# Filter network of the long convolution: its own transfer semaphore, sample columns on two partition halves, weight sums on GpSimd, modulation steps behind the first units

## What is computed

```python
def implicit_filter_fft(length, w1, b1, w2, b2, w3, freq):
    z = jnp.concatenate([t, jnp.cos(bands * w), -jnp.sin(bands * w)], axis=-1)      # length x 33
    hid = jnp.sin(fr * (z @ w1 + b1))
    hid = jnp.sin(fr * (hid @ w2 + b2))
    filt = (hid @ w3).reshape(length, 2, HYENA_ORDER, D_HYENA)
    filt = filt * window[:, None, None, :]
    fwd, bwd = filt[:, 0], filt[:, 1]
    two_sided = jnp.concatenate([fwd, zeros, bwd[1:][::-1]], axis=0)
    two_sided = two_sided / jnp.sum(jnp.abs(two_sided), axis=0, keepdims=True)
    return jnp.fft.rfft(two_sided, axis=0)

def ada_mod(cond, w_ada, b_ada):
    return jnp.split(jax.nn.silu(cond) @ w_ada + b_ada, N_MOD, axis=-1)             # 1024 x 6144
```

## Time and profile before

| | |
|---|---|
| median of 3 runs | 3439.83 us (3432.54 to 3440.22) |
| the profiled execution | 3434.03 us, span 3432.1 us |
| TensorE busy, share of the span | 3190.5 us, 93% |
| VectorE busy | 2245.4 us, 65% |
| ScalarE busy | 1697.3 us, 49% |
| GpSimd busy | 397.4 us, 12% |
| the chain that ended last | matmuls of the experts' stage, from the end back |
| last instruction of the `filters` stage | ends near 350 us |
| first matmul of `projection` | 351.66 us |

### The profile page before, as it was taken

The page is one execution under the profiler, slowest core; times in us unless marked ns, Lnnn a source line. Parts: engine busy times, 40 slices in busy tenths (PEclk is TensorE's granted clock), DMA queues, the critical chain, the costliest instruction groups (busy, mean ns, idle before and its releaser), DMA issues.

```text
span 3432.1 us, 54507 instructions
## 1 busy us (share of the span) xinstructions
PE 3190.5 (93%) x22416; PEld 2468.7 (72%) x22416; DVE 2245.4 (65%) x2850; ACT 1697.3 (49%) x2194; POOL 397.4 (12%) x326
## 2 busy tenths in 40 slices
PE   4879799979899894999999999999999999999996
PEld 2546688868787783777777777777777777777774
DVE  6765423247766637777777777777777777777766
ACT  2222422136511322666666666666666666666664
POOL 1320010011155032000000000000000000000010
PEclk8789899989999996999999999999999999999998
DMA  3455262245378424677877787788778777777785
GB/s 133 162 188 188 102 164 87 79 126 141 142 267 277 144 92 166 261 284 288 294 277 287 278 295 276 272 296 288 275 289 296 273 291 293 275 292 274 277 332 199
DMA packets 226036, 791.15 MB, mean 231 GB/s; under 512 B 28526, under 2 KB 35322, under 8 KB 221565
## 3 DMA queue, kind: packets, MB, share of 16 engines
q1 hardware_dynamic: 206028, 722.02, 57.0%
q0 software_dynamic: 19760, 65.65, 6.7%
HBM read 730.31 MB, written 57.26 MB: 229 GB/s over the span
## 4 chain that ended last, share of the span: by engine, by line
PE 58%; DMA 1%; DVE 1%; ACT 0%; issue 0%; POOL 0%; SPq 0%; ACTq 0%; POOLq 0%; DVEq 0%
PE exp_bank L2860 15%; PE exp_bank L2862 14%; PE exp_bank L2861 14%; PE exp_bank L2870 14%; PE exp_bank L2842 1%; DMA out_y<-exp_xb 1%; PE exp_bank L2844 1%; DMA exp_xb<-residual 0%; PE exp_bank L2828 0%; DVE g_pick L2423 0%; DVE g_pick L2422 0%; DVE g_pick L2425 0%; DVE exp_lo L2556 0%; DMA exp_xq<-hidden_rows,g_rows_q 0%; PE exp_bank L2832 0%
## 5 line engine op out<-in xcount | busy, mean ns | idle before, releaser
L2556 DVE TENSOR_TENSOR exp_lo<-exp_raw,exp_hi 128x1024 fp32r<-128x1024 f32 x1056 | 1277.0, 1223 | 251.2 <-ACT exp_hi L2552 193.6
L2552 ACT ACTIVATE exp_hi<-exp_raw 128x1024 fp32r<-128x1024 f32 x1056 | 1119.4, 1062 | 570.7 <-PE exp_bank L2862 558.0
L2860 PE MATMUL exp_bank<-exp_hi,exp_xt 128*128 128x512 f32 (+1 forms) x1536 | 588.8, 383 | 1.6 <-DVE exp_xt L2709 1.0
L2862 PE MATMUL exp_bank<-exp_hi,exp_xt 128*128 128x512 f32 (+1 forms) x1536 | 572.1, 372 | 0.0
L2861 PE MATMUL exp_bank<-exp_lo,exp_xt 128*128 128x512 f32 (+1 forms) x1536 | 571.7, 372 | 0.0
L2860 PEld LDWEIGHTS exp_bank<-exp_hi,exp_xt 128*128 128x128 f32 x1536 | 289.5, 189 | 87.5 <-issue 39.1
L2862 PEld LDWEIGHTS exp_bank<-exp_hi,exp_xt 128*128 128x128 f32 x1536 | 289.8, 189 | 52.0
L2870 PE MATMUL exp_bank<-exp_raw,exp_xtp 128*32 128x256 f32 (+1 forms) x6144 | 324.1, 363 | 0.0
L2861 PEld LDWEIGHTS exp_bank<-exp_lo,exp_xt 128*128 128x128 f32 x1536 | 290.3, 189 | 45.5
L2860 PE MATMUL exp_bank<-exp_hi,exp_hid 128*128 128x512 f32 x704 | 283.3, 402 | 10.4 <-DVE exp_lo L2556 10.4
L2870 PEld LDWEIGHTS exp_bank<-exp_raw,exp_xtp 128*32 128x32 f32 x6144 | 185.1, 110 | 127.0 <-issue 30.9
(11 more groups left out here) (414 smaller groups left out, 4568.6 us busy)
## 6 DMA issues: line engine op xcount, KB each, us to landing
exp_raw<-in_w SPq DMA_DIRECT2D x1056, 512.0 KB, 6.5
hy_table<-in_basis_s POOLq DMA_DIRECT2D x64, 512.0 KB, 4.7
carry_tiles<-in_w_ada SPq DMA_DIRECT2D x24, 1024.0 KB, 5.4
proj_raw<-in_w_in SPq DMA_DIRECT2D x24, 512.0 KB, 4.6
filt_raw<-in_kbasis_s SPq DMA_DIRECT2D x18, 512.0 KB, 6.1
spectrum_s<-filt_spec SPq DMA_DIRECT2D x34, 256.0 KB, 2.2
carry_flex<-spectrum_s SPq DMA_DIRECT2D x16, 512.0 KB
features<-proj_xr SPq DMA_DIRECT2D x12, 512.0 KB, 3.0
```

What stands on the lines that cost most here:

```text
L2552: act.activation(st.hi[:, n % st.ns, :], raw(n), ACT.Copy).then_inc(st.hi_done, 1)
L2556: dve.tensor_tensor(st.lo[:, n % st.ns, :], raw(n), st.hi[:, n % st.ns, :].bitcast(F32), ALU.subtract).then_inc(st.lo_done, 1)
L2860: pe.matmul(out, xh, wh, start=(k == 0), stop=False)
L2862: mm = pe.matmul(out, xl, wh, start=False, stop=(k == nk - 1))
```

## The change

- Six transfers (`z`, `w1`, the biases twice, `w2` twice) go first and count on `s_net` of their own, `cond` on `s_cond`; then `w3`, then the other nine on `s_in`.
- `w2` has its two copies one below the other, [128, 64] for [64, 128]. The network's prompt columns stay on 64 partitions in both layers. The sample columns' first 512 go to partitions 0 to 63, the last 512 to partitions 64 to 127, so each step covers 512 elements on 128 partitions. ScalarE puts them back beside each other in the second layer's sine, and copies by three blocks.
- GpSimd forms `wsum` and rows 0 to 63 of `W2`; ScalarE makes the zeros of `W2` by a copy with scale 0.
- TensorE's steps ahead of `gen(0)` are gone from there: one stands behind `gen(0)`, one behind `gen(1)`, two ahead of `gen(2)`. VectorE's: one behind `larger(0)`, one behind `larger(1)`, and as before one behind `inverse(0)`. All later calls are as before.
- SP waits for six sines instead of four ahead of the `skip` loads.

```diff
-        w1, w2 = ph.sb("w1", [33, 64]), ph.sb("w2", [64, 128])
+        w1, w2 = ph.sb("w1", [33, 64]), ph.sb("w2", [128, 64])
...
-            sp.dma_start(z, a["z"]).then_inc(s_in, 16)
-            sp.dma_start(w1[:], a["filt_w1"]).then_inc(s_in, 16)
+            sp.dma_start(z, a["z"]).then_inc(s_net, 16)
+            sp.dma_start(w1[:], a["filt_w1"]).then_inc(s_net, 16)
             for x in range(2):
-                sp.dma_start(w2[:, 64 * x:64 * x + 64], a["filt_w2"]).then_inc(s_in, 16)
-                sp.dma_start(fb[64 * x:64 * x + 64, :], a["filt_b"]).then_inc(s_in, 16)
-            for dst, name in ((cond, "cond"), (bada, "bada"), (g["gains"], "gains"), (g["ident"], "ident"), (sel, "sel"), (sgn_f, "sgn")):
+                sp.dma_start(fb[64 * x:64 * x + 64, :], a["filt_b"]).then_inc(s_net, 16)
+            for x in range(2):
+                sp.dma_start(w2[64 * x:64 * x + 64, :], a["filt_w2"]).then_inc(s_net, 16)
+            sp.dma_start(cond[:], a["cond"]).then_inc(s_cond, 16)
+            for x in range(2):
+                sp.dma_start(w3[64 * x:64 * x + 64].rearrange("p d o f -> p (d o f)"), a["filt_w3"]).then_inc(s_w3, 16)
+            for dst, name in ((bada, "bada"), (g["gains"], "gains"), (g["ident"], "ident"), (sel, "sel"), (sgn_f, "sgn")):
                 sp.dma_start(dst[:], a[name]).then_inc(s_in, 16)
             for x, s in enumerate("ps"):
                 sp.dma_start(wmid[:, x, :], a[f"wmid_{s}"]).then_inc(s_in, 16)
                 sp.dma_start(rowf[:, x, :], a[f"rowf_{s}"]).then_inc(s_in, 16)
-            for x in range(2):
-                sp.dma_start(w3[64 * x:64 * x + 64].rearrange("p d o f -> p (d o f)"), a["filt_w3"]).then_inc(s_w3, 16)
...
-            sp.wait_ge(s_sin, 4)
+            sp.wait_ge(s_sin, 6)
...
+            def hidden_p(layer):
+                if layer:
+                    pe.wait_ge(s_sin, 1)
+                pe.matmul(pf[0][0:64, 0:ZS - ZP], w2[0:64] if layer else w1[:], (hid[0:64] if layer else z)[:, ZP:ZS],
+                          start=True, stop=True).then_inc(s_h, 1)
+
+            def hidden_s(layer):
+
+                for h in range(2):
+                    rows, out = slice(64 * h, 64 * h + 64), pf[1 + layer][64 * h:64 * h + 64, :]
                     if layer:
-                        pe.wait_ge(s_sin, 1 if b == 0 else 2)
-                    pe.matmul(pf[b][0:128 if layer else 64, 0:c1 - c0], (w2 if layer else w1)[:],
-                              (hid[0:64] if layer else z)[:, c0:c1], start=True, stop=True).then_inc(s_h, 1)
+                        pe.wait_ge(s_sin, 2)
+                        mm = pe.matmul(out, w2[rows], hid[rows, ZS:ZS + 512], start=True, stop=True)
+                    else:
+                        mm = pe.matmul(out, w1[:], z[:, ZS + 512 * h:ZS + 512 * h + 512], start=True, stop=True)
+                mm.then_inc(s_h, 1)
...
-            pe.wait_ge(s_in, 16 * 16)
-            hidden(0, (0, 1, 2))
-            ada(2)
-            hidden(1, (0,))
-            hidden(1, (1, 2))
+            pe.wait_ge(s_net, 16 * 6)
+            hidden_p(0)
+            hidden_s(0)
+            hidden_p(1)
+            hidden_s(1)
+            pe.wait_ge(s_in, 16 * 9)
+            gen(0)
             ada()
-            gen(0)
             gen(1)
+            ada()
             sums(0)
             middles()
             close(0)
-            ada()
+            ada(2)
             gen(2)
...
-            act.wait_ge(s_in, 16 * 16)
-            act.activation(sgn[:], sgn_f[:], ACT.Copy)
+            act.wait_ge(s_cond, 16)
             act.activation(sc[:], cond[:], ACT.Silu).then_inc(s_silu, 1)
-            for layer in range(2):
-                for b, (c0, c1) in enumerate(((ZP, ZS), (ZS, ZN))):
-                    act.wait_ge(s_y, 2 * layer + b + 1)
-                    part = hid[0:128 if layer else 64, c0:c1]
-                    act.activation(part, y[0:128 if layer else 64, c0:c1], ACT.Sin).then_inc(s_sin, 1)
-                    if layer:
-                        act.wait_ge(s_sin, 3 + b)
-                        act.activation(hs[:, c0:c1], part, ACT.Copy).then_inc(s_hh, 1)
-                if layer == 0:
-                    act.wait_ge(s_ws, 2)
-                    act.activation(W1[:], wsum, ACT.Copy).then_inc(s_wh, 1)
+            for part, (rows, c0, c1) in enumerate(((64, ZP, ZS), (128, ZS, ZS + 512))):
+                act.wait_ge(s_y, part + 1)
+                act.activation(hid[0:rows, c0:c1], y[0:rows, c0:c1], ACT.Sin).then_inc(s_sin, 1)
+            act.wait_ge(s_ws, 2)
+            act.activation(W1[:], wsum, ACT.Copy).then_inc(s_wh, 1)
+            act.activation(W2[64:128], wsum[64:128], ACT.Copy, scale=0.0).then_inc(s_wz, 1)
+            act.wait_ge(s_y, 3)
+            act.wait_ge(s_h, 3)
+            act.activation(hid[0:64, ZP:ZS], y[0:64, ZP:ZS], ACT.Sin).then_inc(s_sin, 1)
+            act.wait_ge(s_sin, 3)
+            act.activation(hs[0:64, ZP:ZS], hid[0:64, ZP:ZS], ACT.Copy).then_inc(s_hh, 1)
+            act.wait_ge(s_y, 4)
+            act.wait_ge(s_h, 4)
+            for h in range(2):
+                c0 = ZS + 512 * h
+                act.activation(hid[0:64, c0:c0 + 512], y[64 * h:64 * h + 64, ZS:ZS + 512], ACT.Sin).then_inc(s_sin, 1)
+            for h in range(2):
+                c0 = ZS + 512 * h
+                act.wait_ge(s_sin, 4 + h)
+                act.activation(hs[0:64, c0:c0 + 512], hid[0:64, c0:c0 + 512], ACT.Copy).then_inc(s_hh, 1)
+            act.wait_ge(s_in, 16 * 9)
+            act.activation(sgn[:], sgn_f[:], ACT.Copy).then_inc(s_sin, 1)
...
+            pool.wait_ge(s_w3, 32)
+            pool.tensor_tensor(wsum[:, :, 0, :], w3[:, 0], w3[:, 1], ALU.add).then_inc(s_ws, 1)
+            pool.tensor_tensor(wsum[:, :, 1, :], w3[:, 1], w3[:, 0], ALU.subtract).then_inc(s_ws, 1)
+            pool.wait_ge(s_wh, 1)
+            pool.tensor_tensor(W2[0:64], wsum[0:64], W1[0:64].bitcast(F32), ALU.subtract).then_inc(s_wl, 1)
...
+                np_, c0, c1 = ((64, ZP, ZS), (128, ZS, ZS + 512))[part]
+                bank = pf[1 + layer if part else 0]
                 yy, kx = y[0:np_, c0:c1], kk[0:np_, c0:c1]
+                dve.wait_ge(s_h, 2 * layer + part + 1)
+                if layer:
+                    dve.wait_ge(s_sin, part + 1)
+                else:
+                    dve.wait_ge(s_h, 2)
+                chain(dve.tensor_scalar(yy, bank[0:np_, 0:c1 - c0], fb[0:np_, layer:layer + 1], fb[0:np_, 2:3], ALU.add, ALU.mult))
...
-            dve.wait_ge(s_in, 16 * 16)
-            reduced(0, 0)
-            reduced(0, 1)
-            dve.wait_ge(s_w3, 32)
-            dve.tensor_tensor(wsum[:, :, 0, :], w3[:, 0], w3[:, 1], ALU.add).then_inc(s_ws, 1)
-            dve.tensor_tensor(wsum[:, :, 1, :], w3[:, 1], w3[:, 0], ALU.subtract).then_inc(s_ws, 1)
-            ada(2)
-            reduced(1, 0)
-            reduced(1, 1)
-            dve.wait_ge(s_wh, 1)
-            dve.tensor_tensor(W2[0:64], wsum[0:64], W1[0:64].bitcast(F32), ALU.subtract).then_inc(s_wl, 1)
-            dve.tensor_tensor(W2[64:128], wsum[64:128], wsum[64:128], ALU.subtract).then_inc(s_wl, 1)
-            for b, (c0, c1) in enumerate(((ZP, ZS), (ZS, ZN))):
-                dve.wait_ge(s_hh, b + 1)
-                dve.tensor_tensor(hs[64:128, c0:c1], hid[64:128, c0:c1], hs[64:128, c0:c1].bitcast(F32), ALU.subtract).then_inc(s_hl, 1)
-            ada()
-            dve.wait_ge(s_wl, 2)
+            dve.wait_ge(s_net, 16 * 6)
+            for layer in range(2):
+                reduced(layer, 0)
+                reduced(layer, 1)
+            for x, (c0, c1) in enumerate(((ZP, ZS), (ZS, ZS + 512), (ZS + 512, ZN))):
+                dve.wait_ge(s_hh, x + 1)
+                dve.tensor_tensor(hs[64:128, c0:c1], hid[0:64, c0:c1], hs[0:64, c0:c1].bitcast(F32), ALU.subtract).then_inc(s_hl, 1)
+            dve.wait_ge(s_in, 16 * 9)
+            dve.wait_ge(s_wl, 1)
+            dve.wait_ge(s_wz, 1)
             windowed(0)
             larger(0)
+            ada()
             for c in range(2):
                 st.split_lo(dve, 0, c)
             windowed(1)
             low(0)
             larger(1)
+            ada()
```

22 lines of the change are left out of this document (5 added, 17 removed).

## The result

The changed kernel is slower: 3485.8 us in the median of four runs (3482.89 to 3488.74), against 3439.77 for the kernel before (3432.54 to 3440.22), 46.0 more. The ratio is 1.0139, with a 95% interval from 1.0121 to 1.0156. The profiled execution took 3482.9, its span is 3481.0; before, it was 3432.1.

A forecast was written before the change was run, and what follows sets the result against it. It took TensorE to bound the filter stage's loop of spectrum jobs, and VectorE's chain its start. 64.5 lost and 14 won gave +50.5 on the profiled 3434.0: 3484.5, left at 3485, range 3455 to 3513.

The forecast's parts named there:

- First matmul: Network's start: with six transfers on `s_net`, TensorE begins at 5.5 us instead of 9.88, 4.4 earlier.
- Two halves in different column groups: Network's sample columns: TensorE's halves run side by side, 1.7 us together; VectorE's simple steps take 0.42, multiply-adds 0.69.
- sharing costs a factor of 1.85: Network's start: GpSimd's sums and VectorE slow each other by 1.85; full sharing puts `windowed(0)` at 34.8, 33 taken.
- gen(2), windowed(2): Unit 2: TensorE's step waits for reciprocal and `ada_out(2)`; `windowed(2)` 4.0 us later, its window's transfer perhaps 1 or 2 more.
- First spectra, windowed(4), close(1): Before the first sample loop: late modulation steps cost 5.4 us at `spectrum_out(0,0,0)`, 5 at `windowed(4)`, 4 to 5 at `close(1)`.
- First sample loop: TensorE's steps wait for `ada_out` of the same slot; 1.6 + 10 + 7 + 1.6 + 7 = 27 us lost.
- the surcharge for slow passes: First sample loop: TensorE runs slow for some microseconds behind a long stall, put at 2.5 to 3 us.
- Behind the loop: At `spectrum_out(1,0,0)` a slow step and job come between, 5.5 us; the next slot costs 1 to 2: 7 lost.
- Second loop: Second sample loop, steps 18 to 23: waits of 2.2 us at even j, 1.6 at odd j, 11.5 lost.
- Rival D: Second sample loop: stalls keep TensorE at its lower clock through six jobs, 23 us more, 3508; chance 0.14.
- The argument against it: Second sample loop: stalls of 2.2 us and shorter are less than the 3.19 behind which rows show slow passes.
- The wait of `filt_pa`: TensorE's `ada_sum` matmul newly waits for VectorE's copy to `g_pick`, some 20 times, near 50 us in total.

The follow-up runs named there:

- the first experiment: Changed kernel with two `ada_out` instead of one behind `inverse(0)` on VectorE; 3424.27 us, ratio 0.9971 to the kernel before.
- the second: Kernel before with only VectorE's `ada_out` behind `inverse(0)` taken away; 3500.19 us, ratio 1.0182.
- the third experiment: Changed kernel with VectorE's missing `ada_out` made up behind `windowed(9)`, just ahead of the second sample loop; 3473.4 us in one run.

## Why the prediction was right, point by point

The time came out as forecast, 3485.8 for 3485, and its cause is the forecast one: experiments 1 and 2 show that one missing `ada_out` makes most of the loss, some 62 of 65 us by either. The sizes were less good than the sum. The stage grew by 50.1 us for the 50.5 forecast, but the medians only by 46.0: the forecast had put its 50.5 on the profiled execution, which lay 5.8 below the median, and that choice, too, brought it nearer to the measured time.

- **First matmul** 5.43 (forecast 5.5). **Two halves in different column groups**: VectorE began at 8.42 (8.5), its simple steps take 0.43 and a multiply-add some 0.71 (0.42 and 0.69). The halves were not undone by themselves; this is read from the trace alone.
- **GpSimd.** `windowed(0)` came at 33.57 (33), but the step "sharing costs a factor of 1.85" was wrong in kind. The earlier trace rows had been read as a slowdown in proportion; the 2.25 for 1.22 fits one turn of GpSimd added to each VectorE instruction as well (GpSimd's two instructions there took 2.24 each, for 1.28 alone), and that row cannot tell the two apart. By the factor, a simple step of 0.43 would have taken 0.8, not 2.5 or 3.8, and GpSimd's 1024 elements 4.6, not 2.33. Too much on GpSimd and too little on VectorE happened to cancel. The forecast said that no row shows one-input steps suffering; they do. The page "SBUF — State Buffer" of the Trainium skill, section "SBUF: two separate sides", says that the port pair is locked for a whole instruction and the other engine is fully blocked; the traces agree with that part (a step of 0.43 took 2.45 and ended 0.29 us behind GpSimd's).
- **gen(2), windowed(2)**: 6.9 lost (forecast 4.0, and 1 or 2 for the window). `gen(2)` started 6.6 us behind the end of `close(0)`, where it had been 2.65, which is the forecast 4.0; the window's transfer, which landed at 80.7, gave the other 3.0: mis-sized. But the 4.0 is not the missing call's, as the forecast had it. It comes from two steps standing ahead of `gen(2)`, the second of which waits for the copy behind the reciprocal: the first experiment put the call in and kept it, the second took the call out of the kernel before and had none of it (4.77 from the reciprocal to `windowed(2)` in both).
- **First spectra, windowed(4), close(1)**: 4.5, 6.7, 2.8 (forecast 5.4, 5, 4 to 5). With the previous point 20.9 for 19.
- **First sample loop**: 17.7 (forecast 27), the largest miss. Take TensorE from its first job to the end of `gen(8)`: 132.47 to 226.89 before, 138.63 to 252.13 after, 19.1 longer. Its idle time there went from 7.5 to 21.5, so 14.0; its busy time for the same 429 matmuls from some 86.8 to 91.95, so 5.2 of slower passes (granted clock 0.93 and 0.88); and VectorE made up 1.4 before `windowed(8)`. The slots were right in kind: waits of 1.31, 5.16, 4.52, 5.08, 1.31 and 4.18, together 21.6, where the forecast had stalls of 1.6, 5.6, 4.6, 5.6, 1.6 and 6.4, together 25.4. What failed most is the surcharge for slow passes, put at 2.5 to 3 behind each of four long stalls, some 10 in all. The old idle stretches at `sums` had slow passes behind them too; they went with those stretches, and the balance is 5.2.
- **Behind the loop**: 11.75 (forecast 7). The row at 268.80 shows 16.67 us of wait, in place of an idle stretch of 15.32 that TensorE had before, but at another place. Before, TensorE had done the step behind `gen(8)` and the matmuls of two prompt jobs (28 matmuls, to 232.04) ahead of that stretch; now all of them come behind it, one job after the other. The forecast had counted the step and one job (5.5) and put 1 to 2 on the rest, which was 6.4.
- **Second loop**: 14.9 (forecast 11.5). The forecast had waits alone, and they were 10.2; 9.0 of the 14.9 is idle time, the other 5.9 are slower passes, which the forecast had put at nothing. Rival D was right that these stalls lower the clock (0.95 to 0.90), and wrong in price, 23 for 5.9. The argument against it, that a stall of 2.2 is shorter than any behind which the rows show slow passes, does not hold: in the third experiment the loop without them has 0.97.
- **The wait of `filt_pa`**: 20 times as forecast, 75.3 us in all for "near 50". The list counts also the 8.53, 6.12 and 6.65 before the loop and the 16.67 behind it, which stand for other waits of before; the forecast had added up little beyond the loops.

The errors of the loss, +1.9, -9.3, +4.75 and +3.4, add up to 0.75, and the gain was 0.75 more than forecast, so the sum stayed where it was; this was luck. A forecast made of the same slots with honest bounds on each (17 to 27, 7 to 12, 10 to 15) would reach over some 20 us, within the range given. What stays open: how much each slot of the first loop adds by itself, since no kernel removed the lag there alone.
